# A decoder trunk on one core: first chunk of each stage on unscaled rows, step-size products moved, last norm ahead of the overflow test, pair loop written out

## What is computed

```python
def rmsnorm(x, g):
    return x * lax.rsqrt(jnp.mean(x * x, axis=-1, keepdims=True) + EPS) * g

for l in range(2):
    h = rmsnorm(x, norm_mix_g[l])
    z = h @ w_in[l]              # split into the inputs of four mixers; z_ddt are 8 columns (step sizes)
    ...                          # gating MLP, pooling, RWKV-7, Mamba-2 SSD
    x = x + merged @ w_out[l]
    h = rmsnorm(x, norm_ffn_g[l])
    if l == 0: x = x + (silu(h @ wg) * (h @ wu)) @ wd         # D_FF 3584
    else:      x = x + moe_swiglu(h, router, wg, wu, wd)      # top 2 of 8 experts, D_FF 3584
return rmsnorm(x, norm_final_g)
```

## Time and profile before

| | us |
|---|---|
| median of 3 runs (2070.4 to 2073.14) | 2070.72 |
| the profiled execution, own time | 2076.29 |
| its span, first to last instruction | 2074.4 |
| PE busy | 2026.7 |
| DVE busy | 1492.8 |
| ACT busy | 1183.1 |
| stream loads, share of the 16 DMA engines over the span | 63.9% |

### The profile page before, as it was taken

How to read it: one execution, slowest core, us unless ns; L and a number is a source line. 1 busy time by engine, 2 the same in 40 slices (tenths; PEclk the granted TensorE clock), 3 DMA queues, 4 the chain that set the end, 5 groups by cost and what they waited for, 6 DMA issues and landing times.

```text
span 2074.4 us, 32408 instructions
## 1 busy us (share of the span) xinstructions
PE 2026.7 (98%) x12814; PEld 1670.4 (81%) x12814; DVE 1492.8 (72%) x1465; ACT 1183.1 (57%) x1073; POOL 54.1 (3%) x56
## 2 busy tenths in 40 slices
PE   8999999899999999999999999999999999999997
PEld 7988889899998989889977677777776777777775
DVE  3757655656544566754768898888888888898886
ACT  3536444433333436434547777777767777677774
POOL 0200000000000020011000000000000000000000
PEclk9999999999999999999989999999999999999998
DMA  7423223445554433223449999899989999999994
GB/s 281 183 102 122 103 98 131 176 164 184 186 190 150 175 130 123 102 87 118 163 144 363 371 359 367 316 368 369 358 342 342 369 362 364 343 356 367 362 366 161
DMA packets 70789, 503.96 MB, mean 243 GB/s; under 512 B 8320, under 2 KB 8576, under 8 KB 9984
## 3 DMA queue, kind: packets, MB, share of 16 engines
q1 hardware_dynamic: 69792, 499.03, 63.9%
q10 hardware_dynamic: 864, 2.95, 0.4%
HBM read 500.90 MB, written 1.05 MB: 242 GB/s over the span
## 4 chain that ended last, share of the span: by engine, by line
PE 57%; DVE 2%; ACT 1%; issue 0%; DVEq 0%; ACTq 0%
PE g L503 37%; PE m L503 19%; PE m L1159 1%; DVE ring_low L2046 1%; PE m L766 0%; DVE ring_low L2104 0%; ACT we_high L1523 0%; PE m L547 0%; DVE h L2364 0%; DVE arena L1954 0%; ACT arena L1259 0%; DVE rstd L2362 0%; DVE mg_low L2082 0%; DVE rstd L1924 0%; PE m L1152 0%
## 5 line engine op out<-in xcount | busy, mean ns | idle before, releaser
L2104 DVE TENSOR_TENSOR ring_low<-ring,we_high 128x2048 fp32r<-128x2048 f32 x336 | 765.5, 2289 | 128.5 <-ACT we_high L1523 127.9
L1523 ACT ACTIVATE we_high<-ring 128x2048 fp32r<-128x2048 f32 x334 | 640.8, 1918 | 269.8 <-PE g L503 171.7
L503 PE MATMUL g<-we_high,hg_high 128*96 128x512 f32 x896 | 357.2, 399 | 3.3 <-DVE ring_low L2104 3.3
L503 PE MATMUL g<-ring_low,hg_high 128*96 128x512 f32 x896 | 354.1, 395 | 0.0
L503 PE MATMUL g<-h_high,ring_low 128*128 128x256 f32 x1248 | 353.0, 283 | 0.0
L503 PE MATMUL g<-we_high,hg_low 128*96 128x512 f32 x896 | 352.8, 394 | 0.0
L503 PEld LDWEIGHTS g<-h_high,ring_low 128*128 128x128 f32 x1248 | 236.4, 189 | 0.0
L503 PE MATMUL g<-h_high,w_high 128*128 128x256 f32 x736 | 208.5, 283 | 7.0 <-DVE h L1709 6.8
L503 PE MATMUL g<-h_low,w_high 128*128 128x256 f32 x736 | 208.4, 283 | 0.0
L503 PEld LDWEIGHTS g<-we_high,hg_low 128*96 128x96 f32 x896 | 144.9, 162 | 63.8
L503 PEld LDWEIGHTS g<-we_high,hg_high 128*96 128x96 f32 x896 | 145.2, 162 | 63.2 <-DVE ring_low L2104 4.2
(11 more groups left out here) (314 smaller groups left out, 3165.3 us busy)
## 6 DMA issues: line engine op xcount, KB each, us to landing
ring<-stream SPq DMA_DIRECT2D x472, 1024.0 KB, 4.8
sw<-sw_in SPq DMA_DIRECT2D x1, 1088.0 KB, 11.2
sw<-sw_in ACTq DMA_DIRECT2D x1, 1088.0 KB, 8.3
x<-x_in SPq DMA_DIRECT2D x4, 256.0 KB, 4.9
out<-h ACTq DMA_DIRECT2D x4, 256.0 KB, 2.1
cc<-cc_in SPq DMA_DIRECT2D x1, 816.5 KB, 12.1
rep<-rep_in SPq DMA_DIRECT2D x1, 768.0 KB, 13.6
rep<-rep_in ACTq DMA_DIRECT2D x1, 768.0 KB, 8.5
```

The source lines that it names most:

```text
L503: return pe.matmul(o, a, b, start=start, stop=stop, skip_group_check=True)
L1523: A(we_high[n % 3][:, :], ring[:, slot, :], ACT.Copy).then_inc(high_ready, 1)
L2104: TT(ring_low[:, slot, :], ring[:, slot, :], we_high[n % 3][:, :], ALU.subtract).then_inc(low_ready, 1)
```

## The change

Four edits, told by what they do:

1. Unscaled rows. DVE writes xg = x * gain (without rstd) before the root is known: at the start from x as loaded, in the last stage of layer 0's merge, and in the last part of the FFN. PE multiplies chunk 0 of both input projections and of the FFN by xg, in fp32; DVE then multiplies that result by rstd (`scale`). Chunk 0 of the FFN is therefore no longer split; the buffers of w_high shift by one, and chunk 1 of the FFN runs its three passes one after the other (`rounded_first`).
2. Step-size products stand ahead of chunk 1; their small weights sw have a semaphore of their own.
3. Final norm (`last_norm`, `last_sum`) stands ahead of the flag's test; in the overflow case it is done again.
4. The pair loop of PE alone is written out (`for` in place of `Fori`); ACT, DVE and SP keep their loops.

```diff
@@ project (PE)
+                    if n == 1:
+                        step_rows(l)
+                    if n == 2:
+                        pe.wait_ge(layer_in, 16 * (l + 1))
+                        pe.wait_ge(all_consts_in, 32)
...
                         for k in range(DT):
-                            pe.wait_ge(h_ready, 2 * DT * l + k + 1)
+                            if k % 2 == 0:
+                                pe.wait_ge(S["xg_ready"], 8 * l + k // 2 + 1)
                             for j in range(2):
-                                last = mm(gb((name, i))[:, j * T:(j + 1) * T], w[:, DT * j + k, :], h[:, k, :], k == 0 and j == 0, k == DT - 1)
+                                last = mm(gb((name, i))[:, j * T:(j + 1) * T], w[:, DT * j + k, :], xg[:, k, :], k == 0 and j == 0, k == DT - 1)
...
-                    if n == 1:
-                        pe.wait_ge(layer_in, 32 * (l + 1))
-                        pe.wait_ge(all_consts_in, 32)
-                        m_free(pe, l, "dt")
...
@@ step_rows (PE)
+                pe.wait_ge(layer_sw_in, 16 * (l + 1))
+                m_free(pe, l, "dt")
+                for k in range(DT):
+                    pe.wait_ge(h_ready, 2 * DT * l + k + 1)
+                    last = mm(mb("dt")[0:H, 0:T], sw[:, SW["dt"] + H * k:SW["dt"] + H * (k + 1)], h[:, k, :],
+                              k == 0, k == DT - 1)
@@ ffn_split (PE)
+                w = chunk(FFN0)
+                for k in range(DT):
+                    if k % 2 == 0:
+                        pe.wait_ge(S["xg_ready"], 4 + k // 2 + 1)
+                    for j in range(2):
+                        last = mm(gbank[0][:, j * T:(j + 1) * T], w[:, DT * j + k, :], xg[:, k, :], k == 0 and j == 0, k == DT - 1)
+                last.then_inc(chunks_used, 1)
...
+                    for k in range(DT):
+                        if k % 2 == 0:
+                            pe.wait_ge(S["h_split_high"], 4 + k // 2 + 1)
+                        for j in range(2):
+                            mm(o(j), wh[:, DT * j + k, :], h_high[:, k, :], k == 0 and j == 0, False)
+                    pe.wait_ge(low_ready, NS + 1)
...
@@ experts (PE)
-                with pe.Fori(0, E // 2 - 1) as pair:
+                for pair in range(E // 2 - 1):
@@ end of the program (PE)
+            last_sum(0)
+            overflow = pe.value_load(flag[0:1, 0:1], min_val=0, max_val=1)
+            with pe.If(overflow > 0):
+                pe.wait_ge(m_drained[0], L * M_TOTAL[0] + 1)
+                again()
...
@@ evacuate (ACT)
                     if name == "zg":
+                        if i == 0:
+
+                            act.wait_ge(S["zg_scaled"], l + 1)
+                            two = zg[:, 0:2, :]
@@ dense (ACT)
-                    A(sil[:, s % 7, :], gbank[s % 4][:, 0:T], ACT.Silu).then_inc(silu_done, 1)
-                    high(s + 2)
+                    if s == 0:
+                        high(2)
+                        act.wait_ge(S["gu_scaled"], 1)
+                        A(sil[:, 0, :], first_gu[:, 0:T], ACT.Silu).then_inc(silu_done, 1)
+                    else:
+                        A(sil[:, s % 7, :], gbank[s % 4][:, 0:T], ACT.Silu).then_inc(silu_done, 1)
+                        high(s + 2)
@@ around norm2 (ACT)
-                    high(0)
+                    high(1)
...
-                    high(1)
@@ end of the program (ACT)
+            last_norm(0, lambda i: act.wait_ge(S["back_drained"], 4 * E + i + 1))
+            act.wait_ge(S["flag_ready"], 1)
+            overflow = act.value_load(flag[0:1, 0:1], min_val=0, max_val=1)
...
@@ new helpers (DVE)
+            def unscaled(l, name, i):
+
+                for k in (2 * i, 2 * i + 1):
+                    ins = V.tensor_scalar(xg[:, k, :], x[:, k, :], par(l, name, k), None, ALU.mult)
+                    (q.add(ins, S["xg_ready"]) if k % 2 else q.add(ins, v_seq))
+
+            def scale(dst, bank, done):
+
+                two = lambda ap: ap.rearrange("p (j t) -> p j t", j=2)
+                q.add(TT(dst, two(bank[:, :]), over(rstd[:, :], 2), ALU.mult), done)
@@ merge (DVE)
-                    if l == 1:
-                        g_done(dve, l, unit)
...
+                    g_done(dve, l, unit)
+                    unscaled(l, "norm_ffn", i)
@@ dense (DVE)
-                    low(n + 1)
+                    if n:
+                        low(n + 1)
+                    else:
+                        dve.wait_ge(chunks_used, FFN0 + 1)
+                        scale(first_gu.rearrange("p (j t) -> p j t", j=2), gbank[0], S["gu_scaled"])
...
-                dve.wait_ge(ffn_drained, FT + 4)
+                    dve.wait_ge(ffn_drained, FT + i + 1)
+                    unscaled(1, "norm_mix", i)
@@ main order (DVE)
+                if l == 0:
+                    for i in range(4):
+                        dve.wait_ge(x_loaded[i], 16)
+                        unscaled(0, "norm_mix", i)
                 norm(lambda: m_done(dve, l, "norm1"), lambda k: par(l, "norm_mix", k), h_ready)
                 z_low(l, 1)
                 for i in range(4):
                     split_h(2 * l, i)
+                dve.wait_ge(chunks_used, chunk0(l) + 1)
+                scale(zg[:, 0:2, :], gb(("zg", 0)), S["zg_scaled"])
...
-                    low(0)
+                    low(1)
...
+            last_norm(0)
+            overflow = dve.value_load(flag[0:1, 0:1], min_val=0, max_val=1)
```

More of the change, by code:

```diff
@@ new lines, in ffn_split, with rounded_first @@
+                last.then_inc(chunks_used, 1)
+                for i in range(4):
+                    pe.wait_ge(m_drained[i], M_TOTAL[i])
+                def rounded_first():
+                    o = lambda j: gbank[1][:, j * T:(j + 1) * T]
+                    wh, wl = high[0], low[(FFN0 + 1) % RING]
+                    for k in range(DT):
[4 more added lines that the diff above has]
+                    pe.wait_ge(low_ready, NS + 1)
+                    for k in range(DT):
+                        for j in range(2):
+                            mm(o(j), wl[:, DT * j + k, :], h_high[:, k, :], False, False)
+                    for k in range(DT):
+                        if k % 2 == 0:
+                            pe.wait_ge(S["h_split"], 4 + k // 2 + 1)
+                        for j in range(2):
+                            last = mm(o(j), wh[:, DT * j + k, :], h_low[k // 4][:, k % 4, :], False, k == DT - 1)
+                    return last
@@ L973, in ffn_split @@
+                for s in range(1, FT):
+                    if s == 1:
+                        pe.wait_ge(high_ready, NS + 1)
+                    else:
+                        pe.wait_ge(low_ready, NS + s)
                     if s >= 4:
                         pe.wait_ge(ffn_drained, s - 3)
[L976 to L986, removed]
+                    if s == 1:
+                        last = rounded_first()
+                        last.then_inc(chunks_used, 1)
+                        continue
@@ L987, in ffn_split @@
+                    for j in range(2):
+                        for k in range(DT):
+                            last = three(gbank[s % 4][:, j * T:(j + 1) * T], high[(s + 1) % 2][:, DT * j + k, :],
+                                         low[(FFN0 + s) % RING][:, DT * j + k, :], h_high[:, k, :], h_low[k // 4][:, k % 4, :],
+                                         k == 0, k == DT - 1)
                     last.then_inc(chunks_used, 1)
@@ L995, in ffn_split @@
                     for d in range(DT):
-                        last = three(mbank[d // 2][:, (d % 2) * T:(d % 2 + 1) * T], high[n % 2][:, (k % 2) * DT + d, :],
+                        last = three(mbank[d // 2][:, (d % 2) * T:(d % 2 + 1) * T], high[(n + 1) % 2][:, (k % 2) * DT + d, :],
                                      low[(FFN0 + n) % RING][:, (k % 2) * DT + d, :], gu_high[:, k, :], gu_low[:, k, :],
@@ L1228, in _, with last_sum @@
                     experts()
[L1229 to L1238, removed]
+            def last_sum(n):
+                for j in range(DT):
+                    if j % 2 == 0:
+                        pe.wait_ge(sq_ready, 4 * (2 * L + n) + j // 2 + 1)
+                    last = mm(mbank[3][:, 0:T], ones, sq_last[:, j, :], j == 0, j == DT - 1)
+                last.then_inc(m_filled[0], 1)
+            last_sum(0)
[3 more added lines that the diff above has]
+                again()
+                with pe.Fori(0, E) as e:
+                    overflowed(e)
+                last_sum(1)
         @block.scalar
```

108 lines of the change are left out of this document (54 added, 54 removed).

## The result

The changed kernel took 2051.14 us in the median of five runs (2050.26 to 2056.42), the kernel before 2070.72 in five runs on the same chip (2065.16 to 2073.14): a ratio of 0.991 (95% interval 0.990 to 0.993). It is faster by 19.6 us in the medians. The profiled execution took 2050.26 us around a span of 2048.2, at a mean clock of 0.994. I had forecast 2045.1 us (2040 to 2052) from a sum of 25.6 us: the direction was right, the size was 6 us too large.

What follows compares the result with a forecast made beforehand. TensorE (PE), busy 98% of the span, was taken as the bound, through its idle and lower-clock time. Terms 5.9 + 6.1 + 4.4 + 3.8 + 5.4 = 25.6 us, off the 2070.72 median, gave 2045.1 us (range 2040 to 2052).

Steps and rivals of the forecast that it cites:

- Layer 0, 5.9: Input projection of layer 0: chunk 0 on unscaled rows starts at the sum's end; chunk 2 starts 5.9 us earlier.
- layer 1, 4.4: Input projection of layer 1: chunk 0 follows the sum of squares without pause; chunk 2 starts at 672.8 for 677.20, 4.4 us.
- FFN, 6.1: FFN: chunk 0 starts at the sum's end, PE then waits 2.1 us for chunk 2's low half; 6.1 us gained.
- the clock rival: FFN: the clock falls in the new 2.1 us wait, costing 1.4 to 2.9 us; 2046.5 to 2048.0 us, chance 0.30.
- Edges, 3.8: Expert pair loop: each of two jumps back on PE costs 1.91 us; writing its loop out returns 3.8 us.
- End, 5.4: Final norm ahead of the overflow test: last sum starts at 2057.3 without long pause, ends at 2060.9; 5.4 us gained.
- the forecast of nothing for the tests behind the last work: Kernel end: overflow tests cost between 0 and 3.1 us; taken as 0 because the last output transfer is still landing.
- The mixers absorb the head start: Rival, layers' mixers: a DVE chain, not PE, sets their end; gain 15.3 us, time 2055.4 us, chance 0.04.
- Written-out code starves PE: Rival, expert pairs: instruction fetches for straight code stall PE's sequencer, 52 us; time 2100.9 us, chance 0.02.
- The pauses at the edges are not the jumps and stay: Rival, loop edges and last sum: neither returns anything; gain 16.4 us, time 2054.3 us, chance 0.04.

## Why the prediction was right or wrong

- **Layer 0, 5.9; layer 1, 4.4: right.** Measured 6.2 and 4.6. Chunk 0 at the sum's end, full clock through it, step products as cover. Undoing the parts shows what they carry: 4.8 to 5.0 us are lost without the unscaled rows, and 1.8 with them but without the products ahead of chunk 1. The price of the clock depends on the execution: chunk 0 of layer 0 took 10.11, 10.13 and 8.80 us in three of the kernel before and 8.61 with its pause put back, 1.5 to 3.1 more than the 7.07 of full clock. By the third of these the gain of layer 0 is 4.8 us (21.0 from the sum's end to chunk 2, for 16.2). So the mechanism is shown, and that 5.9 met 6.2 to 0.3 us is in part luck: the forecast took the clock of one execution, and the comparison used the same one.
- **FFN, 6.1: chain right, 4.6 measured, and the clock rival came true.** The wait was 1.87 us for 2.1. The rival (chance 0.30) said that the clock falls in it, for 1.4 to 2.9 us. In nine of the twelve executions profiled in which this wait is found the FFN stretch took 247.2 us, in three 245.7. Without the fall the gain is 251.8 - 245.7 = 6.1, the forecast to a tenth; with it 4.6. What I had wrong was that the sum priced the clock behind this wait at nothing, and its chance at 0.30: the nearest rows, 3.0 us of idle, were all followed by the lower clock, and 1.87 us usually was. It is worth 1.5 us.
- **Edges, 3.8: wrong, 0.6 measured.** This is the step that failed: the sentence "ACT, DVE and SP keep their loops; where they jump, they have work in flight", which put the cost of DVE's jump at nothing. It took what DVE did in the kernel before as a property of the jump. In the kernel before it was right: DVE's loop was not fetched again. The change itself put 26 instructions ahead of that loop (DVE has x1465 instructions on the page before and x1491 after), and with that each turn fetched code anew, DVE issued nothing for 4.84 us at the first edge, and PE lost 1.5 to 1.7 us there and at the second. I had asked what longer code does to PE and not what added code does to an engine that keeps its loop. PE's own term was sized right: with DVE out of the way both edges are 23.9, and 1.91 each is there.
- **End, 5.4: right.** 5.6 to the last root, 0.3 given back between the root and the end. In the other kernels with this end that last stretch is 0 to 1.1 us longer than before, so the forecast of nothing for the tests behind the last work was a little low.
- **The rivals.** "The mixers absorb the head start" was wrong: the stretches of both layers gained at least what their starts did, in the mean of all executions too (6.8 and 5.0 us). "Written-out code starves PE" was wrong: no gap on PE beyond the waits above. "The pauses at the edges are not the jumps and stay" names the right outcome at the edges for a wrong reason: that low half was late this time because DVE's own code was.
- **The sum against the median.** The median of 2051.14 lies at the upper end of the range. By stages 21.3 us came back of 25.6: 3.2 are missing at the edges, 1.5 in the FFN and 0.1 at the end, and the layers gave 0.5 more than forecast. The medians differ by 19.6. The remaining 1.7 us are less than what the same kernel varies by from run to run, 6 to 8 us. The size of the clock's share in layer 0 was read from one execution with a clock of 0.986, 5.6 us above the median, and the sum taken from the median; the executions of the same kernel at 0.988 and 0.989 were 1.6 and 3.1 us shorter, so that such a draw is high. The two profiled executions differ by 26.2 us, near my 25.6, but 4.9 of that lie in no changed place: their agreement is luck.

"Runtime: NRT & Kernel Launch" of the Trainium skill, Instruction fetch mechanics, says that a taken branch whose target is outside a window of two pages forces a fetch before execution goes on. The edges agree in kind: DVE's jump is free or costs a stall of 4.5 to 4.8 us of issue with packets on the queue of its code, by where the code lies. How far back a jump reaches without a fetch, no run here shows. The price of a branch in "Advanced Engine Details and Errata", Control Flow Timing, some 108 ns, may hold for a jump that fetches nothing, for which the edges of 23.9 us show no cost; for one that fetches, the measured 4.84 us decides.

## What to carry to other kernels

The price of a loop can depend on where it lies in its engine's code; here DVE's did. After an edit, compare the packets of each instruction queue with those before, and if they rose by the same number at every turn, shift or write out the loop; a few idle instructions ahead of it can be worth microseconds. Where several engines jump at the same place, count the stall of each: they can hide one another, and removing one alone then shows nothing. And take a sum only from stretches that several executions share, since the clock's draw in one execution is as large as the terms.

## What was not expected of the hardware

- 28, 56, 84 or 96 more instructions ahead of DVE's loop, or 18 fewer, all make the two edges 3.3 us shorter together. The kernel after happened to sit at the one bad place of the six tried. How wide that place is was not measured. The packets are of some 8 KB (0.20 MB / 25), and a turn brings five of them or none. My guess is that the loop's code touches one such block more at the bad place than at the others; no run shows it, and how many blocks an engine holds was not measured either.
- PE's jumps brought 4 packets more on its own queue (108 for 104) in the kernel with PE's loop back; whether PE's loop has a free place too was not tried.
- The clock falls after the FFN's wait of 1.87 us in nine of twelve executions, and the stretch is then 1.5 us longer.
